# A two-block network on one core: the first block's values multiplied from X as it lands, the norm applied behind, and one VectorE step moved in both mixers

## What is computed

```python
x = x + parallel_mixer(rms_norm(x, g_mix[l]), w_in[l], ...)
# in parallel_mixer
z = h @ w_in
q, k, v, o, gates, gu, gv = jnp.split(z, cuts, axis=-1)
# in rms_norm
y = xf * lax.rsqrt(jnp.mean(xf * xf, axis=-1, keepdims=True) + RMS_EPS)
return (y * g.astype(jnp.float32)).astype(x.dtype)
# in _pool_mixer, for each of four windows
wsum = cs[:, w:w + L] - cs[:, :L]
groups.append(wsum / count[None, :, None] - xg)
```

## Time and profile before

| | |
|---|---|
| median of 3 runs | 1599.45 us (1598.53 to 1599.94) |
| the profiled execution, its own time | 1598.25 us |
| its span | 1596.4 us |
| PE busy | 1558.0 us, 98% of the span |
| DVE, ACT, POOL busy | 952.6, 692.8, 63.8 us |
| granted TensorE clock, mean | 0.999 |
| DMA | 398.87 MB, 250 GB/s over the span |

### The profile page before, as it was taken

How to read it: one execution, slowest core, us unless ns; L and a number is a source line. 1 busy time by engine, 2 the same in 40 slices (tenths; PEclk the granted TensorE clock), 3 DMA queues, 4 the chain that set the end, 5 groups by cost and what they waited for, 6 DMA issues and landing times.

```text
span 1596.4 us, 22640 instructions
## 1 busy us (share of the span) xinstructions
PE 1558.0 (98%) x9209; PEld 1178.2 (74%) x9209; DVE 952.6 (60%) x1636; ACT 692.8 (43%) x1229; POOL 63.8 (4%) x68
## 2 busy tenths in 40 slices
PE   7999999999999999999999999999999999999998
PEld 6997885443433433448997889999899978899997
DVE  5967655222333233237788667766767885677666
ACT  6765542111010110136664446554655644465544
POOL 1010000000000000003001000000030010000000
PEclk9999999999999999999999999999999999999999
DMA  9443477999999999996345545555453445455550
GB/s 367 170 148 132 177 324 297 410 423 424 423 424 423 422 424 424 424 420 214 133 146 179 179 160 214 186 186 187 169 185 133 172 158 184 173 198 185 185 185 27
DMA packets 57246, 398.87 MB, mean 250 GB/s; under 512 B 6352, under 2 KB 6736, under 8 KB 10036
## 3 DMA queue, kind: packets, MB, share of 16 engines
q1 hardware_dynamic: 56706, 395.63, 64.2%
q10 hardware_dynamic: 434, 1.77, 0.3%
HBM read 396.33 MB, written 1.05 MB: 249 GB/s over the span
## 4 chain that ended last, share of the span: by engine, by line
PE 84%; DMA 10%; DVE 4%; ACT 2%; issue 1%; SPq 0%; DVEq 0%; ACTq 0%
PE P L172 82%; DMA ew<-in_ws_dram 8%; PE P L175 2%; DMA ez<-in_ws_dram 1%; DVE RINGL L184 1%; ACT WH L178 0%; DMA RING<-in_ws_dram 0%; DVE LA L190 0%; SPq L217 0%; ACT HA L178 0%; DVE SM L190 0%; DVE YB L184 0%; DVE PXP L190 0%; ACT JNK L178 0%; ACT L181 0%
## 5 line engine op out<-in xcount | busy, mean ns | idle before, releaser
L184 DVE TENSOR_TENSOR RINGL<-RING,WH 128x1024 fp32r<-128x1024 f32 x347 | 421.9, 1240 | 104.7 <-ACT WH L178 103.4
L178 ACT ACTIVATE WH<-RING 128x1024 fp32r<-128x1024 f32 x351 | 356.5, 1053 | 49.9 <-PE P L172 47.5
L172 PE MATMUL P<-HA,WH 128*128 128x256 f32 x1208 | 345.4, 286 | 0.0
L172 PE MATMUL P<-LA,WH 128*128 128x256 f32 x1208 | 340.3, 282 | 0.0
L172 PE MATMUL P<-HA,RINGL 128*128 128x256 f32 x1208 | 340.3, 282 | 0.0
L172 PEld LDWEIGHTS P<-HA,WH 128*128 128x128 f32 x1208 | 227.7, 189 | 5.6 <-issue 3.0
L172 PEld LDWEIGHTS P<-HA,RINGL 128*128 128x128 f32 x1208 | 228.4, 189 | 1.9
L172 PEld LDWEIGHTS P<-LA,WH 128*128 128x128 f32 x1208 | 228.6, 189 | 0.0
L172 PE MATMUL P<-WH,HA 128*128 128x512 f32 x368 | 148.1, 402 | 1.8 <-ACT VN L178 1.3
L172 PE MATMUL P<-RINGL,HA 128*128 128x512 f32 x368 | 145.7, 396 | 1.8 <-POOL RINGL L184 1.4
L172 PE MATMUL P<-WH,LA 128*128 128x512 f32 x368 | 144.9, 394 | 0.5 <-DVE LA L190 0.4
(11 more groups left out here) (411 smaller groups left out, 2431.6 us busy)
## 6 DMA issues: line engine op xcount, KB each, us to landing
RING<-in_ws_dram SPq DMA_DIRECT2D x279, 1024.0 KB, 4.9
ew<-in_ws_dram SPq DMA_DIRECT2D x42, 1024.0 KB, 23.6
ez<-in_ws_dram SPq DMA_DIRECT2D x15, 1024.0 KB, 20.5
ek<-in_ws_dram SPq DMA_DIRECT2D x11, 1024.0 KB, 18.2
ef<-in_ws_dram SPq DMA_DIRECT2D x8, 1024.0 KB, 12.8
eha<-in_ws_dram SPq DMA_DIRECT2D x4, 1024.0 KB, 9.3
ela<-in_ws_dram SPq DMA_DIRECT2D x3, 1024.0 KB, 6.9
ewr<-in_ws_dram SPq DMA_DIRECT2D x3, 1024.0 KB, 13.8
```

Of the source, the lines that this page charges most:

```text
L172: return self.engine.matmul(*a, **k) if self.engine else self
L178: return self.engine.activation(*a, **k) if self.engine else self
L184: return self.engine.tensor_tensor(*a) if self.engine else self
```

## The change

It has two parts.

**First block.** PE turns X by plain transposes (`raw_turn`, which the kernel has already) as it lands, without the root, and HB and LB take X times the gain (`first_hi`, `first_lo`). The eight steps of the values use these. They go chunk by chunk, in the order (0,0), (1,0), (0,1), (1,1), (2,0), (2,1), (3,0), (3,1) of (chunk, tile), with the turn of the second tile behind the first step. ACT multiplies by the root when it empties the values' banks (`scalar_values`). For the gates and all that follows, the normalised operand is made beside this: PE spreads the roots over a row (`spread_root`) behind step (2,0), ACT copies them to RB0, DVE multiplies the four banks by gain and root into QK (`first_normal`, 16 instructions), ACT rounds to HA (four), POOL subtracts into LA (four of 128x512), and no longer makes the low half of chunk 1, which is DVE's. The gain moves from PARS to the first 136 columns of CONS, units 0 and 1 come in halves, and PARS comes behind them.

```diff
-LOW_ON_POOL = {1, 3} | {B2 + l * L_CHUNKS + L_AT["ffn"] + 12 for l in range(2)}
+LOW_ON_POOL = {3} | {B2 + l * L_CHUNKS + L_AT["ffn"] + 12 for l in range(2)}
@@ fetch
-    if u == U_B2:
+    if u in (0, 1, U_B2):
         w = m.slot[m.home[u]]
-        e.dma_start(w[:, 0:1024], A["ws"][u][:, 0:1024]).then_inc(*s.first_in.up(0))
+        e.dma_start(w[:, 0:1024], A["ws"][u][:, 0:1024]).then_inc(*(s.second_in if u == 1 else s.first_in).up(u))
@@ new
+def first_hi(e, m, s, t, i):
+    e.wait_ge(*s.turned["raw mix", t, i])
+    for q in range(4):
+        k = 4 * i + q
+        e.activation(m.HB[:, k, t * 128:(t + 1) * 128], m.P[4 + 2 * t + i][:, q * 128:(q + 1) * 128], ACT.Copy,
+                     scale=m.con("gain", k, k + 1)).then_inc(*s.norm_hi.up("raw mix", t, k))
...
+def first_normal(e, m, s, t, i):
+    ta = slice(t * 128, (t + 1) * 128)
+    e.wait_ge(*s.evac["spread", "mix"])
+    for q in range(4):
+        k = 4 * i + q
+        p = e.scalar_tensor_tensor(m.QK[:, k, ta], m.P[4 + 2 * t + i][:, q * 128:(q + 1) * 128],
+                                   m.con("gain", k, k + 1), m.RB0[:, ta], ALU.mult, ALU.mult)
+    p.then_inc(*s.normal.up(t, i))
+def first_normal_hi(e, m, s, t, i):
...
+    e.activation(m.HA[:, 4 * i:4 * i + 4, ta], m.QK[:, 4 * i:4 * i + 4, ta],
+                 ACT.Copy).then_inc(*s.norm_hi.up("mix", t, i))
+def first_normal_lo(e, m, s, t, i):
...
+    e.tensor_tensor(m.LA[:, 4 * i:4 * i + 4, ta], m.QK[:, 4 * i:4 * i + 4, ta],
+                    plain(m.HA[:, 4 * i:4 * i + 4, ta]), ALU.subtract).then_inc(*s.normal_lo.up(t, i))
@@ gpsimd_start
-    lo_half(e, m, s, 1)
     lo_half(e, m, s, 3)
+    first_normal_lo(e, m, s, 0, 0)
+    first_normal_lo(e, m, s, 1, 0)
+    first_normal_lo(e, m, s, 0, 1)
+    first_normal_lo(e, m, s, 1, 1)
@@ scalar_mixer
+    first_hi(e, m, s, 0, 0)
+    hi_halves(e, m, s, 0, 2)
+    first_hi(e, m, s, 0, 1)
     mean_square(e, m, s, "mix", 0, 0)
...
+    mean_square(e, m, s, "mix", 1, 0)
+    first_hi(e, m, s, 1, 0)
+    rstd_root(e, m, s, "mix", 0)
+    rstd_root(e, m, s, "mix", 1)
+    hi_half(e, m, s, 2)
+    first_hi(e, m, s, 1, 1)
+    hi_halves(e, m, s, 3, 5)
+    e.wait_ge(*s.product["spread", "mix", 1])
+    e.activation(m.RB0[:, :], m.P[m.bank["spread", "mix"]][:, 0:256], ACT.Copy).then_inc(*s.evac.up("spread", "mix"))
+    hi_half(e, m, s, 5)
+    first_normal_hi(e, m, s, 0, 0)
+    first_normal_hi(e, m, s, 1, 0)
+    scalar_values(e, m, s, 0)
+    first_normal_hi(e, m, s, 0, 1)
+    first_normal_hi(e, m, s, 1, 1)
+    hi_half(e, m, s, 6)
@@ scalar_values
-                 ACT.Copy).then_inc(*s.evac.up("v", t))
+                 ACT.Copy, scale=m.SM[:, 12 + t:13 + t]).then_inc(*s.evac.up("v", t))
@@ vector_layer
-    lo_until(e, m, s, c + 5)
     vector_pool(e, m, s, l, 3)
     e.wait_ge(*s.stream[c])
     e.tensor_tensor(m.LRT[:, :], m.P[m.bank[c]][:, 0:256], m.RB[:, :], ALU.mult).then_inc(*s.scaled.up("lr", l))
+    lo_until(e, m, s, c + 5)
```

More of the change, by code:

```diff
@@ L53 @@
 _n = 0
-for _name, _w in [("ident", 128), ("ones", 128), ("le", 128), ("ge", 128), ("lt", 128),
+for _name, _w in [("ident", 128), ("gain", 8), ("ones", 128), ("le", 128), ("ge", 128), ("lt", 128),
                   ("mf", 128), ("mb", 128), ("onehot", 512), ("iota", 64), ("cf", 130), ("cb", 130),
@@ L253 @@
 XS = 256 ** -0.5
[L255 to L258 removed]
+CON_WIDTH = {"iota": 64, "onehot": 512, "cf": 130, "cb": 130, "m2": 64, "edge": 64, "gain": 8, "lrone": 1}
+LOW_ON_POOL = {3} | {B2 + l * L_CHUNKS + L_AT["ffn"] + 12 for l in range(2)}
 EXTRA = ("ek1", "egs", "ez", "ef2", "ef1", "ext", "eha", "ela", "ew0", "ew1", "ew2", "ewr")
@@ L363, in __init__ @@
         self.DN = z("DN", [128, 4])
+        self.RB0 = z("RB0", [128, 128 * 2])
         self.QX = at("QX", [128, 4, 256], Z + 16384)
@@ L650, in hi_half @@
 def hi_half(e, m, s, c):
-    e.wait_ge(*(s.first_in[0] if c == B2 else s.landed[m.home[c // 2]][c // 2]))
+    e.wait_ge(*(s.second_in[1] if c == 2 else s.first_in[c // 2] if c in (0, B2) else s.landed[m.home[c // 2]][c // 2]))
     if c >= B2 + NH or NH <= c < B2:
@@ L935, in sync_start @@
     fetch(e, m, s, A, 1)
+    e.dma_start(m.CONS[:, 136:264], A["con"][:, 136:264]).then_inc(*s.ones_in.up(0))
+    e.dma_start(m.PARS[:, :], A["par"]).then_inc(*s.par_in.up(0))
     fetch(e, m, s, A, 2)
@@ L976, in tensor_mixer @@
 def tensor_mixer(e, m, s):
[L977 to L984, removed]
+    raw = normed(s, "raw mix", m.HB, m.LB)
+    v = lambda j, t: stream_tile(e, m, s, 0, j, t, raw, (s.evac, ("v", t)))
+    e.wait_ge(*s.ident_in[0])
+    raw_turn(e, m, s, "mix", 0, [(s.x_in, (0,))] * 2)
+    v(0, 0)
+    raw_turn(e, m, s, "mix", 1, [(s.x1_in, (0,))] * 2)
+    for t in range(2):
+        for i in range(2):
+            m.free[4 + 2 * t + i] = [(s.normal, (t, i))]
+    v(1, 0)
+    v(0, 1)
+    v(1, 1)
+    v(2, 0)
+    e.wait_ge(*s.ones_in[0])
+    spread_root(e, m, s, "mix", 3)
+    v(2, 1)
+    v(3, 0)
+    v(3, 1)
+    a = Operand(m.HA, m.LA, lambda k, t: (s.norm_hi, ("mix", t, k // 4)), lambda k, t: (s.normal_lo, (t, k // 4)))
     stream_t(e, m, s, 4, a, (s.evac, ("gate", 3)))
@@ L1439, in vector_mixer @@
         rstd_end(e, m, s, "mem", t)
-        rstd_diagonal(e, m, s, "mem", t, (s.turned, ("mix", t, 1)))
+        rstd_diagonal(e, m, s, "mem", t, (s.product, ("spread", "mix", t)))
     lo_half(e, m, s, 11)
@@ L4383, in vec @@
         par[:v.shape[0], PAR[name]:PAR[name] + v.shape[1]] = v
-    for n in ("g_mix", "g_mem", "g_xattn", "g_moe", "g_head", "conv_w", "conv_b"):
+    con = constants()
+    con[:, CON["gain"]:CON["gain"] + 8] = I["g_mix"][0].reshape(8, 128).T
+    for n in ("g_mem", "g_xattn", "g_moe", "g_head", "conv_w", "conv_b"):
         vec(n, I[n][0])
```

85 lines of the change are left out of this document (46 added, 39 removed).

## The result

| | before | changed |
|---|---|---|
| median of 20 runs each | 1599.06 us (1597.78 to 1600.35) | 1601.5 us (1599.43 to 1604.23) |
| ratio, 95% interval | | 1.0016 (1.001 to 1.0022) |
| span of the profiled execution | 1596.4 us | 1598.1 us |
| its granted clock, mean | 0.999 | 0.997 |

The change makes the kernel about 2.4 us slower. The forecast was 0.4 us faster; 1601.5 lies inside the range given, and within the 0.2% called "no change", but the interval excludes 1. So the forecast was wrong in sign, and there are 2.8 us to find.

A forecast was written before the change was run, and what follows sets the result against it. PE was taken to bound the kernel, so head changes carry to the end undiminished. Head +1.5 and pooled sum -1.9 gave -0.4 us: 1597.85 on the profiled execution, 1599.0 against the 1599.45 median; range 1595.3 to 1602.5.

The forecast's parts named there:

- The pooled part: Pooled sum in both layers: a DVE low half moved behind it, W2A 0.9 us earlier a layer, 1.9 in all.
- The collisions: At the head, DVE and POOL exclude each other: tile 1's column steps held to 19.5, POOL's LA pieces to 31.2.
- chunk 5: Mark for the head: its products on PE were to begin at 32.4, 1.5 us later than 30.88 in the kernel before.
- POOL keeps the ports: Rival: POOL runs its four LA pieces without DVE between; head 0, total -1.9, 1597.6 us; chance 0.13.
- the collisions don't cost: Rival: DVE's steps come before POOL's start at the head; head -2.2, total -4.1, 1595.3 us; chance 0.23.
- PE falls back to the low clock: Rival: PE's waits at the head drop its clock; 2.9 us lost, total +2.5, up to +6.6; chance 0.15.
- When the clock rises: PE's high clock after 5.8 us of work: from transposes 10.2, chunk 5 at 31.9; from products 14.7, chunk 5 at 32.4.
- the landing of unit 0's first half: Weights for the first values: taken to land at 6.5 us, bounded by 6.3 and 7.5; PE's first product at 7.6.

The follow-up runs named there:

- steps_first: The changed kernel with DVE's low half of chunk 2 put behind both tiles' root steps, scales and DIAGs; ratio 1.0002 (0.9993 to 1.0011).
- pool_only: The kernel before with only the low half moved behind the last pooled sum and LRT, both layers; ratio 0.999, 1597.81 us against 1599.22.
- both_again: Repeat timing: changed kernel, DVE doing both tiles' column steps before chunk 2's low half, and the last two LA pieces; ratio 0.9976, 1596.1 us.
- both_whole: The changed kernel with DVE's column steps before chunk 2's low half, DVE making the last two LA pieces, and unit 0 in one transfer; ratio 0.9984.

## Why the prediction was wrong

**The pooled part (-1.9): right.** -0.91 and -0.92 by the starts, 1.4 us measured alone, with 1.9 in its interval (0.9981 to 0.9999).

**The collisions: right in kind, place and nearly in size.** The first was forecast to end at 19.5 and ended at 19.67. It hung on 0.08 us of order and not 0.15, and held tile 1's second step and not the first; POOL's last piece was forecast to end at 31.2, with DVE's low halves between the pieces, and ended at 30.95; chunk 5 at 32.4, measured 32.36. The rule of the Trainium skill in "SBUF — State Buffer", section "Who interferes with whom", held: with DVE's low halves kept away, POOL's four pieces took 5.02 us and not 6.95. "POOL keeps the ports" and "the collisions don't cost" are refuted.

**The step that failed is "PE falls back to the low clock", given 0.15.** My own sum had PE waiting from 28.3 to 31.3, "longer than any wait that it had between products before", and I set against it that the kernel before kept the high level through waits of 1 to 1.4 us. That says nothing on a wait of 3, and the term stood at nothing in the sum. After a wait of 2.76 us or more the products ran at the low level in five profiles of six (the sixth is steps_first); after the waits of 1.4 to 2.1 us for POOL near 15 us, in one of four. Its size was forecast as 2.9 us, from the start of the kernel; by the wait's end to chunk 6, less 4.13, it is 1.5 and 2.6 in the two profiles of the changed kernel, 1.2, 2.7 and 1.5 in the other three. The total that this rival gave, +2.5, is close to the +2.4 measured by luck: its 2.9 was too large, and the late landing below, which it did not have, makes up for that. The Trainium skill's page "TensorE: Matmul & The Clock Gate", section "What's actually happening", which I cited for this rival, has PE fall after idling, and the rows agree in kind (2.76 to 3.04 us of idle time). Near 260 us the clock fell behind two waits of 1.1 us with short products between, so the longest single wait is not what to look at alone.

**When the clock rises.** The prediction tried 5.8 us of work, from the transposes or from the products. Neither came out. In the two profiles of the changed kernel the spacing of PE's instructions halves near 12 and near 15 us, some 4 and 5 us behind the first product (8.18, 9.57) and 8 and 11 behind the first transpose (4.30, 4.33). That the rise is free, as the sum has it, was not tested.

**A second term was mis-sized: the landing of unit 0's first half,** "I bound it by 6.3 and 7.5 and take 6.5". It was 7.07 in the first profile and 8.2 to 9.04 in eight others. The first profile reached 32.36 in spite of 7.07 because PE spread tile 1's roots at 20.11 and not at 20.6 as in my sum; two errors cancelled. In the other eight profiles with both halves issued at once the first product comes at 9.3 to 10.2, 9.7 in the mean: the values begin 1.5 us earlier than in the four with the old head (10.86 to 11.58, 11.2 in the mean), where the sum had 3.3 (7.6 against 10.86).

**And the profile of before was an early one.** Its PE starts at 7.42; in the three other profiles with that start it is 7.61, 7.87 and 8.14. By the mean, chunk 6 begins at 34.05 in before and pool_only (33.73, 34.38), and at 38.2 in the three profiles with the changed head (36.73, 38.16, 39.61): +4.1 us. With -1.8 for the pooled part that is +2.3, and 2.4 was measured. Of the 4.1, 1.5 are the collisions as forecast and 1.8 the clock (the mean of 1.5, 2.6 and 1.2); the rest, 0.8, I put down to the later landing, less what the kernel before also varies, and it can hold something of the clock's later rise. This last split is worked out, not measured by itself, and the means are of two and three profiles that differ by 0.7 and 2.9 us.

## What to carry to other kernels

A wait on the engine that bounds the kernel has a second price when it is long: here 2.8 us of waiting for POOL cost 1.2 to 2.7 more in slow products, in five of six profiles. Cutting the longest wait to 1.1 us or filling it took that away. Short waits are not safe in themselves: two of 1.1 us with hardly any work between them cost 1.2 to 1.5 us in 12 of 16 profiles. When an operand is spread over two engines that share a resource, count what each does to the other; here giving DVE two of POOL's four pieces and putting the short steps ahead of the long one turned +2.4 us into -3.3 to -4.8. A forecast that names a wait longer than any seen should not put its price at nothing because shorter ones were free. A start time taken from one profile is one draw: look at other profiles before a sum is built on it, and bound a transfer's landing by the latest seen.

## What the hardware showed that was not expected

- Splitting a transfer did not make its first half land earlier than the whole: 9.04 us for the first half and 10.3 for the second in both_again, 8.99 for the whole unit in both_whole. With the second half held back the first was there by 6.72; in two of ten profiles it was at 7.0 to 7.1 without that.
- An added wait made the kernel 3.5 us faster: POOL's four pieces 5.02 us instead of 6.95, and no fall of the clock at the head.
- The clock fell behind 3.04 us of idle time in a stretch where PE had been busy for 10 us without a gap, and came back some 3 us later; 1.66 us in the same place left it alone. Elsewhere it fell behind 1.87 us in one execution and not behind 2.09 us, or 2.78 us, in others.
- It also fell near 260 us behind waits of 1.07 and 1.11 us with five products of 32 columns between, in 12 of 16 profiles, in kernels of either head, and 14 products then took up to 3.35 us instead of 1.92.
